# Four modulation strips moved from mLSTM and MLA into the second products of the two FFNs

## The reference, cut to what matters

```
for layer in range(2):
    sh1, sc1, g1, sh2, sc2, g2 = split(silu(c) @ mod_w[layer] + mod_b[layer], 6)
    h = rms_norm(x, norm_g[layer, 0]) * (1 + sc1) + sh1
    y = mlstm_mixer(h, ...)            if layer == 0   # chunkwise mLSTM, 4 heads
        mla_mixer(h, ..., shared k, v) if layer == 1   # latent attention, 8 heads
    x = x + g1 * rms_norm(y, norm_g[layer, 1])
    h = rms_norm(x, norm_g[layer, 2]) * (1 + sc2) + sh2
    y = square(relu(h @ w1)) @ w2                      # FFN, 1024 -> 4096 -> 1024
    x = x + g2 * rms_norm(y, norm_g[layer, 3])
```

## Time and profile before

| quantity | value |
|---|---|
| median of 3 runs | 2864.56 us (2861.3 to 2871.22) |
| the profiled execution's own time | 2856.19 us |
| its span in the trace | 2854.6 us |
| TensorE matmul (PE) busy | 2663.9 us, 93% |
| VectorE (DVE) busy | 1939.4 us, 68% |
| ScalarE (ACT) busy | 1059.7 us, 37% |
| GpSimd (POOL) busy | 863.3 us, 30% |
| data moved | 536.83 MB, 188 GB/s on average |

### The profile page before, as it was taken

How to read it: one execution, slowest core, us unless ns; L and a number is a source line. 1 busy time by engine, 2 the same in 40 slices (tenths; PEclk the granted TensorE clock), 3 DMA queues, 4 the chain that set the end, 5 groups by cost and what they waited for, 6 DMA issues and landing times.

```text
span 2854.6 us, 50064 instructions
## 1 busy us (share of the span) xinstructions
PE 2663.9 (93%) x17946; PEld 2258.7 (79%) x17946; DVE 1939.4 (68%) x3229; ACT 1059.7 (37%) x1549; POOL 863.3 (30%) x525
## 2 busy tenths in 40 slices
PE   5988999999999998899999999999988799988898
PEld 4458999999877874679999998778875489755886
DVE  6422997777898774536977778997773579054880
ACT  1214444433434442234444434434441144321443
POOL 2005995000000001047990000000011058810687
PEclk9989999999999998789999999999999899989999
DMA  8524555444467776154555545667876445563454
GB/s 341 214 74 148 170 178 182 160 159 164 167 217 241 273 271 220 36 171 155 177 179 167 161 155 171 207 220 256 274 249 252 175 145 180 193 232 106 148 183 148
DMA packets 147620, 536.83 MB, mean 188 GB/s; under 512 B 16784, under 2 KB 17168, under 8 KB 147232
## 3 DMA queue, kind: packets, MB, share of 16 engines
q1 hardware_dynamic: 115088, 417.08, 43.9%
q0 software_dynamic: 31104, 113.26, 11.4%
q10 hardware_dynamic: 1296, 4.72, 0.4%
HBM read 531.85 MB, written 3.15 MB: 187 GB/s over the span
## 4 chain that ended last, share of the span: by engine, by line
PE 74%; DVE 9%; issue 5%; POOL 4%; DMA 4%; ACT 2%; DVEq 0%; SPq 0%; POOLq 0%; ACTq 0%
PE ps L1596 18%; PE ps L1216 14%; PE ps L602 9%; PE ps L1220 7%; PE ps L2181 5%; POOL split_lo L1271 4%; PE ps L2159 4%; DMA ring<-in_stream 3%; PE ps L1169 3%; PE ps L1554 3%; PE ps L580 2%; PE ps L2163 2%; DVE split_lo L1283 1%; DVE mod_acc L382 1%; PE ps L1753 1%
## 5 line engine op out<-in xcount | busy, mean ns | idle before, releaser
L1258 ACT ACTIVATE split_hi<-ring 128x1024 fp32r<-128x1024 f32 x672 | 708.3, 1055 | 704.3 <-PE ps L1220 447.8
L1271 POOL TENSOR_TENSOR split_lo<-ring,split_hi 128x1024 fp32r<-128x1024 f32 x288 | 745.4, 2601 | 207.1 <-ACT split_hi L1258 206.4
L1283 DVE TENSOR_TENSOR split_lo<-ring,split_hi 128x1024 fp32r<-128x1024 f32 x384 | 468.7, 1221 | 102.4 <-ACT split_hi L1258 102.4
L362 POOL DMA_DIRECT2D mod_w<-in_mod x96 | 50.8, 529 | 1148.2 <-ACT gate L1310 426.5
L1216 PE MATMUL ps<-hT_hi,split_hi 128*128 128x256 f32 x2048 | 292.6, 285 | 4.0 <-ACT split_hi L1258 4.0
L1220 PE MATMUL ps<-hT_hi,split_lo 128*128 128x256 f32 x2048 | 290.0, 284 | 2.4 <-POOL split_lo L1271 2.3
L1216 PE MATMUL ps<-hT_lo,split_hi 128*128 128x256 f32 x2048 | 289.0, 284 | 0.0
L1596 PE MATMUL ps<-split_hi,gate_hi 128*128 128x512 f32 x1024 | 284.9, 399 | 1.1 <-DVE gate_lo L1281 1.1
L1596 PE MATMUL ps<-split_hi,gate_lo 128*128 128x512 f32 x1024 | 276.7, 391 | 2.6 <-DVE gate_lo L1281 2.6
L1596 PE MATMUL ps<-split_lo,gate_hi 128*128 128x512 f32 x1024 | 277.3, 391 | 0.0
L1255 ACT ACTIVATE gate_hi<-gate 128x256 fp32r x256 | 106.9, 418 | 446.0 <-PE ps L1596 446.0
(11 more groups left out here) (318 smaller groups left out, 3771.5 us busy)
## 6 DMA issues: line engine op xcount, KB each, us to landing
ring<-in_stream SPq DMA_DIRECT2D x782, 512.0 KB, 4.1
mod_w<-in_mod POOLq DMA_DIRECT2D x96, 512.0 KB, 4.8
small<-in_mod POOLq DMA_DIRECT2D x80, 512.0 KB, 6.2
gate<-in_mod POOLq DMA_DIRECT2D x32, 512.0 KB, 9.4
gate<-in_mod ACTq DMA_DIRECT2D x8, 512.0 KB, 11.6
gate<-in_mod SPq DMA_DIRECT2D x8, 512.0 KB, 10.2
x_kept<-x POOLq DMA_DIRECT2D x4, 512.0 KB, 4.2
gate<-x_kept POOLq DMA_DIRECT2D x4, 512.0 KB, 8.7
```

The costliest lines, as they stand in the source:

```text
L1258: nc.scalar.activation(split_hi[:, e, :], ring[:, slot, e * D:(e + 1) * D], ACT.Copy).then_inc(hi_made, 1)
L1271: nc.gpsimd.tensor_tensor(split_lo[:, e, :], ring[:, slot, e * D:(e + 1) * D], split_hi[:, e, :].bitcast(F32), ALU.subtract).then_inc(lo_m ...
L1283: nc.vector.tensor_tensor(split_lo[:, e, :], ring[:, (START[name] + j) % RING, e * D:(e + 1) * D], split_hi[:, e, :].bitcast(F32), ALU.sub ...
```

## The change

The side strips get two new stages, `f2_0` and `f2_1`, in the second products of the two FFNs. Strips 21, 26 and 27 leave mLSTM for `f2_0`, and strip 25 leaves MLA for `f2_1`. mLSTM keeps 16 chunks in four groups of four, MLA keeps 16 in groups of 8, 4 and 4. In the second products VectorE makes the remainders (`ffn2_lo_vector`, written out, not a loop) instead of GpSimd, and passes a chunk after three of every four remainders as long as there are any. GpSimd, whose splits end with the first product, issues the new strips' loads there. Sums of strips stand on TensorE's list ahead of given slabs of the second product; the sum of strip 20, whose chunks stay in mLSTM, goes there too, and strip 27's stays at the head of MLA. The preparation of the row moves to behind VectorE's remainders of slab 7, and its matmuls to ahead of TensorE's slab 9.

```diff
-SIDE_STRIPS = {"swa": [10, 11], "ml": [19, 20, 21, 26, 27], "mla": [23, 24, 25]}
+SIDE_STRIPS = {"swa": [10, 11], "ml": [19, 20], "f2_0": [21, 26, 27], "mla": [23, 24], "f2_1": [25]}
@@ mlstm_tensor, end
-            side_sums_tensor(t, "ml", 0, 1, 3)
@@ mlstm_vector: the four groups of chunks
-            side_chunks_vector(v, "ml", 0, 11)
+            side_chunks_vector(v, "ml", 0, 4)
-            side_chunks_vector(v, "ml", 11, 21)
+            side_chunks_vector(v, "ml", 4, 8)
-            side_chunks_vector(v, "ml", 21, 31)
+            side_chunks_vector(v, "ml", 8, 12)
-            side_chunks_vector(v, "ml", 31, 40)
+            side_chunks_vector(v, "ml", 12, 16)
@@ new, ahead of mlp_tensor
+        STRIP_SUMS = [[("ml", 1, 1), ("f2_0", 0, 6), ("f2_0", 1, 12)], [("f2_1", 0, 6)]]
+        ROW_SLAB = 9
+
+        def ffn2_lo_vector(v, l):
+
+            v.eng.wait_ge(lo_made, TILE0[f"ffn2_{l}"])
+            strips = SIDE_STRIPS[f"f2_{l}"]
+            for s in range(4 * MLP_STEPS):
+                for e in range(2):
+                    split_lo_vector(v, f"ffn2_{l}", 0, s, e)
+                    n = 2 * s + e
+                    if n % 4 < 3 and n - n // 4 < DC * len(strips):
+                        side_chunks_vector(v, f"f2_{l}", n - n // 4, n - n // 4 + 1)
+                for stage, m, at_slab in STRIP_SUMS[l]:
+                    if at_slab == s - 1:
+                        side_stores_vector(v, stage, 2, m, m + 1)
+                if s == ROW_SLAB - 2:
+                    post_gain_vector(v, f"f2_{l}", col("norm2", 4 * l + 3), MOD2[l] + G2, 0)
@@ mlp_tensor, second product
-            post_tensor(t, f"f2_{l}", 0)
             def step(i):
                 for j in range(4):
+                    for stage, m, at_slab in STRIP_SUMS[l]:
+                        if at_slab == 4 * i + j:
+                            side_sums_tensor(t, stage, 2, m, m + 1)
+                    if (4 * i + j) == ROW_SLAB:
+                        post_tensor(t, f"f2_{l}", 0)
                     t.eng.wait_ge(hid_made, i * 4 + (l * 16 + j + 1))
@@ mlp_vector
-            else:
-                side_stores_vector(v, "ml", 0, 1, 3)
             parts_vector(v, f"m2_{l}", hT, mlp_hi, mlp_lo, 4, scale_c, MOD2[l] + SH2, f"m2_{l}")
-            post_gain_vector(v, f"f2_{l}", col("norm2", 4 * l + 3), MOD2[l] + G2, 0)
             with v.eng.Fori(0, MLP_STEPS) as i:
...
             v.seen.clear()
+            ffn2_lo_vector(v, l)
             post_rest_vector(v, f"f2_{l}", 0, 4, ("m1_1", None)[l])
@@ mla_tensor, mla_vector
-            side_sums_tensor(t, "ml", 4, 3)
+            side_sums_tensor(t, "f2_0", 4, 2)
-            side_chunks_vector(v, "mla", 0, 10)
+            side_chunks_vector(v, "mla", 0, 8)
-            side_chunks_vector(v, "mla", 10, 14)
+            side_chunks_vector(v, "mla", 8, 12)
-            side_chunks_vector(v, "mla", 14, 24)
+            side_chunks_vector(v, "mla", 12, 16)
@@ GpSimd's list
-            for name in ("ffn1_0", "ffn2_0", "ffn1_1", "ffn2_1"):
-                if name == "ffn1_1":
+            for l in range(2):
+                if l:
                     side_loads_gpsimd(g, "mla")
-                split_lo_gpsimd(g, name, 0, 4)
+                split_lo_gpsimd(g, f"ffn1_{l}", 0, 4)
+                side_loads_gpsimd(g, f"f2_{l}")
```

More of the change, by code:

```diff
@@ L95 @@
 V_STRIPS = [[6, 7, 8, 12, 13, 9], [14, 15, 16, 17, 18, 22]]
-SIDE_STRIPS = {"swa": [10, 11], "ml": [19, 20, 21, 26, 27], "mla": [23, 24, 25]}
+SIDE_STRIPS = {"swa": [10, 11], "ml": [19, 20], "f2_0": [21, 26, 27], "mla": [23, 24], "f2_1": [25]}
 ORDER = (list(range(FIRST_STRIPS)) + V_STRIPS[0] + SIDE_STRIPS["swa"] + V_STRIPS[1] + SIDE_STRIPS["ml"]
-         + SIDE_STRIPS["mla"])
+         + SIDE_STRIPS["f2_0"] + SIDE_STRIPS["mla"] + SIDE_STRIPS["f2_1"])
 assert sorted(ORDER) == list(range(STRIPS))
@@ L403, in side_acc, with side_loads_gpsimd @@
                     return gate[:, at_:at_ + D]
[L405 to L412, removed]
+        def side_loads_gpsimd(g, stage, first=0, last=None):
+            for q in range(first, last or len(SIDE_STRIPS[stage]) * DC):
+                s, k = SIDE_STRIPS[stage][q // DC], q % DC
+                n = SIDE.index(s) * DC + k
+                if n >= 4:
+                    g.wait_ge(*when(f"side{n - 4}"))
+                g.eng.dma_start(side_slots[n % 4], io["mod"][PLACE[s] * DC + k]).then_inc(side_landed[n % 4], 16)
         def side_chunks_vector(v, stage, first, last):
@@ L2373, in mla_vector @@
             double_norm_vector(v, "m1_1", col("norm2", 4), MOD2[1] + SC1, MOD2[1] + SH1,
-                               col("kvn2"), KVMOD2 + 1, 0, False, lambda: side_stores_vector(v, "ml", 4, 3))
-            side_chunks_vector(v, "mla", 0, 10)
+                               col("kvn2"), KVMOD2 + 1, 0, False, lambda: side_stores_vector(v, "f2_0", 4, 2))
+            side_chunks_vector(v, "mla", 0, 8)
             v.wait_ge(*when("mla.ss"))
```

## The result

The changed kernel takes 2875.04 us (median of 20 runs, 2862.91 to 2884.68) against 2863.29 for the one before beside it (20 runs, 2849.91 to 2871.25). The ratio is 1.0045, 95% interval 1.0032 to 1.0058: slower by 9 to 17 us. The forecast was 2875.3, or 1.0037.

The account below looks back on a forecast made before the run. The prediction took TensorE to be the bound in the second products, with ring waits in the mixers. Losses of 19.7 less gains of 9.0 gave +10.7 us on the median of 2864.56: 2875.3 us, range 2859 to 2885.

Parts of the forecast that it names:

- first remainder, behind the last ReLU: Start of an FFN's second product: VectorE finishes its squares first, so the first remainder comes 8.2 us after the ReLU.
- its cost, with the row moved, both FFNs: Start of the second products: TensorE stands 5.4 us waiting for the first remainder, twice, +10.8 us.
- clock behind it: Behind that stall in each FFN: TensorE's clock drops, 1.7 us each, +3.4 us in all.
- four sums: Second products: four strip sums of 1.68 us move to where TensorE is the bound, +6.7 us.
- strips' traffic in the product: Second products: the moved strips' loads beside the weight ring cost 0, bounds 0 and +8 us.
- first ring wait of mLSTM with its clock: mLSTM, first wait for weights: the wait (3.4) and its clock loss (1.66) go, -5.1 us.
- second and third: mLSTM's later ring waits: slightly less competing traffic and half a clock loss saved, together -2.1 us.
- MLA's third: Ring wait in MLA's output product: no strip loads beside it any more, -1.8 us.
- rival of a hidden backlog: Start of the second products: VectorE's backlog is hidden, TensorE's first tile doesn't wait; -14.2, giving 2861 us; chance 0.09.
- Crowding: First FFN's second product: strip loads crowd the weight ring and hold TensorE, +8, giving 2883 us; chance 0.14.
- faster pace of the late v loop: Second products: with VectorE splitting, matmuls go at 0.228 us instead of 0.233; -4.2, giving 2871 us; chance 0.13.
- all ring waits go with the change: mLSTM and MLA: side loads alone cause all ring waits, so 16 us more is gained, giving 2859 us; chance 0.11.

Follow-up runs that it names:

- e4: Changed kernel, but GpSimd makes the remainders of each second product's first four tiles; chunks, sums and row shifted to suit: 2862.81 us, ratio 1.0001 to the kernel before.
- e1: Kernel before, with only the second products' remainders moved from GpSimd to VectorE; strips, sums and row unchanged: 2875.38 us, ratio 1.0048 to the kernel before.
- e3: Changed kernel without TensorE's sums of four strips in the second products; loads and passes stay: 2868.27 us, ratio 1.0025 to the kernel before.
- e5: Changed kernel, with each strip load in the second products cut from 512 KB to 8 KB: 2875.92 us, ratio 1.0043 to the kernel before.
- e6: Changed kernel, with each strip load in mLSTM and MLA cut from 512 KB to 8 KB: 2855.11 us, ratio 0.9965 to the kernel before.
- e7: Changed kernel with MLA and FFN 1 as before; in FFN 0 GpSimd makes the first four remainders, sums and row leave the product: 2858.75 us, ratio 0.9979 to before.
- e8: e7 with mLSTM's sixteen chunks in groups of 4 and 12, strip 19's sum behind the output product: 2853.76 us, ratio 0.9966 to the kernel before.

## Why the prediction held

Sign, size and the main mechanism came out as forecast. By its own steps, in us:

| step | predicted | in the trace | settled by |
|---|---|---|---|
| first remainder, behind the last ReLU | 8.2 | 8.18 | timeline; e4 |
| its cost, with the row moved, both FFNs | +10.8 | +10.8 | timeline; e1, e4 |
| clock behind it | +3.4 | +5.3 (2.7, 2.6) | matmuls, e4 |
| last remainder | -1.2 | -1.2 | timeline |
| four sums | +6.7 | +6.7 | e3 |
| strips' traffic in the product | 0 | about 0 | e5 |
| first ring wait of mLSTM with its clock | -5.1 | -4.5 | chain |
| second and third | -2.1 | about 0 | waits |
| MLA's third | -1.8 | -1.7 in the wait, -0.6 in the stage | waits |

**The stall.** I took VectorE's fast rows for its last three slabs, because GpSimd would be idle then, and that gave the remainder's time to 0.1 us. Its cost in one product: TensorE's first remainder matmul came 4.53 us behind the ReLU before and comes 8.18 behind it now: 3.65, and 1.72 for the row, which is now paid inside the product. That is 5.4, as forecast (3.7 and 1.72 in FFN 1). The cost has two parts that I had not parted: 4.38 of waiting for VectorE, and 1.72 of waiting for ScalarE that the row's matmuls had filled. Moving the row, which I priced at 0 by itself, took the filling away. The rival of a hidden backlog fell: the backlog stood there in full.

**The clock.** This term was mis-sized: 1.7 a dip, read in mLSTM behind a wait of 3.4 us, where this trace has 2.7 and 2.6. No rule for the size comes out of the runs. The same sixteen matmuls, first matmul with a remainder to the start of the next piece, in us:

| run | waits ahead, FFN 0 | time | waits ahead, FFN 1 | time |
|---|---|---|---|---|
| e4 (clock held) | 1.7, 0.3 | 3.84 | 1.7, 0.3 | 3.84 |
| e1 | 0.9, 3.5 | 5.39 | 0.9, 3.6 | 6.46 |
| after | 1.7, 4.4 | 6.54 | 1.7, 4.4 | 6.43 |
| e3 | 1.7, 4.4 | 6.42 | 1.7, 4.4 | 5.40 |
| e5 | 1.7, 4.4 | 5.98 | 1.7, 4.4 | 6.40 |
| e6 | 1.7, 5.0 | 5.34 | 1.7, 5.0 | 5.52 |

So a dip cost 1.5 to 2.7 us. In e1 nearly the same waits were followed by 1.5 and 2.6, and the longest waits, in e6, by 1.5 and 1.7. Hence the 1.7 was one draw from a spread, and the forecast took it for the price; why a dip is long or short is open.

**The gains in the mixers.** Here only what shows in several traces counts. mLSTM's first wait went as worked out (2.8 of 3.4 in idle time, 1.7 in the matmuls): with 40 chunks it is 3.4 and 3.9 us (before, e1), with 16 chunks at most 1.8 (seven traces). The relief of the second and third, 0.2 MB less traffic each by my estimate, is not to be seen: together 6.1 and 5.3 with 40 chunks, 4.7 to 7.8 with 16 in fours. MLA's last wait went: 1.7 to 2.8 with 24 chunks (before, e1, e7, e8), none in the five traces with 16. That the stage gained only 0.6 comes from the wait before it, 2.6 in the trace of before, but 4.0 to 5.2 in the other three with 24 chunks and 3.8 to 5.6 with 16: so the 4.4 is within what this wait does anyway, and is no cost of the change that a run shows. MLA's first, 4.5, which the prediction calls a ring wait, stands in its row as "issue"; that the strips' loads have part in it is shown only by e6, where the longest such wait is 1.8.

**The sum.** The losses in the second products are 21.6 (predicted 19.7) and the gains 5.8 (predicted 9.0); with 0.9 from the FFNs' heads, which vary by as much between traces of one code, this is the +16.7 of the trace. The timed ratio gives 12.9, from 9.2 to 16.6; the forecast of 10.7 lies inside, on the low side, where both misses put it. That the measured median and the forecast are 0.3 us apart is luck, as the kernels' own ranges are some 20 us wide.

**The other rivals.** Crowding fell with e5. The faster pace of the late v loop fell with 0.233 to 0.235 us a matmul in the chain. That all ring waits go with the change fell, but e6 shows that its mechanism is right: without the side loads' traffic mLSTM has none of these waits, and MLA 0.5 us. I had weighed it against the loads that stay, and that was the right reason: four chunks ahead of a slab are enough for a wait of 3.9. The rule of the Trainium skill on SBUF ports (SBUF: State Buffer, section Who interferes with whom), by which the splitter can't set TensorE's pace, agrees with the traces: 0.233 with GpSimd as splitter, 0.233 to 0.235 with VectorE.

**What stays open.** In single traces MLA takes 146.0 to 153.9 us with 24 chunks and 145.4 to 150.1 with 16, so no run here prices its part of the change by itself. Why the clock stays low longer in some executions (mLSTM in e1, the dips above) is not explained either.

## What to carry to other kernels

Moving work to an engine that is busy with the stage's end puts its backlog ahead of the next stage's first operand: work out when that engine reaches the first item, and let the old engine make the first few. Ask of each small thing that is moved away whether it was filling a hole. Traffic that competes with a prefetch belongs where the bound is compute: 24 loads were free inside a compute-bound product, but their sums, on the bounding engine, were not. A price read from a single dip of the clock should stand in a sum as a range.

## What the runs showed of the hardware

- GpSimd's remainders slow VectorE's passes of a slab to a third or less. In e7, with GpSimd splitting, a subtraction on VectorE takes 2.71 us and a cast 2.55; once it stops the same take 0.69 and 0.43. Kernel e7, timeline:

```profile
2406.59 0.68 DVE L2310 TENSOR_TENSOR gate<-gate 128x512 f32<-128x512 f32 x1
2407.28 4.97 POOL L2542 TENSOR_TENSOR split_lo<-ring,split_hi 128x1024 fp32r<-128x1024 f32 x2 [2.25 <-ACT split_hi L1258]
2407.41 2.55 DVE L2312 CAST hid_hi<-gate 128x512 f32 x1
...
2410.09 2.71 DVE L2314 TENSOR_TENSOR hid_lo<-gate,hid_hi 128x512 f32 x1
```

- A stall of TensorE of 3.5 to 5.1 us was followed by 1.5 to 2.7 us of loss at the low clock, in ten cases ahead of the same matmuls (e1, after, e3, e5, e6), without order by its length; after waits of 1.7 and 0.3 us (e4) the granted clock stayed at 1.00.
- mLSTM of unchanged code differs by 10.4 us between two executions (before, e1), with granted clocks of 0.93 and 0.85, while the second products without a stall repeat to 0.2.
